# Scan of the latents: ScalarE writes x times D into the place of y head by head, and VectorE adds both directions to it

## The chip, the cores and the metric

The kernel runs on one core of a Trainium2 chip. The core has TensorE for matrix products (PE in the profile), VectorE (DVE), ScalarE (ACT), GpSimd (POOL) and SyncE (SP, here only an issuer of DMAs). Each engine works through its own list of instructions in order, and they wait for each other on semaphores. The metric is the device time of one execution in microseconds. Three runs of the kernel before took 1609.01 to 1610.98 us, with a median of 1609.97 us.

## The reference, cut to what matters

The model is one layer of a hybrid backbone: attention and a bidirectional state-space scan (Mamba-2) on one projection, then a gated merge and an MLP. 128 context tokens and 512 latent tokens go through it. The change concerns the scan of the latents. For each head the scan gives, per direction, a part within a chunk of 128 tokens and a part that comes from the state carried into the chunk; both directions and a skip term are then summed:

```python
y_diag = einsum('bcgij,bcgrij,bcjgr,bcjgrp->bcigrp', cb, decay, dt, x)
y_off  = einsum('bcign,bcigr,bcgrpn->bcigrp', Cm, exp(acs), h_prev)
y = y_f + flip(y_b) + d_skip[:, None] * xs      # 32 heads of 64 channels
y = rms_norm(y * silu(z), ssd_norm)
```

`d_skip` has one number for each head; `xs` is the convolved x.

## The kernel before, in words

Tokens lie on the 128 partitions in five tiles: chunk 0 is the context, chunks 1 to 4 are the latents. A chunk has 32 heads of 64 channels, so y is 128 x 2048; it is worked on in four quarters q of 8 heads (128 x 512), and each quarter has two groups g of four heads, g = 0 to 7.

The backward states of the latents are made first, and then the loops of the latents run, one on each engine, with c from 1 to 4. TensorE's loop multiplies the scan's small products between pieces of the big input projection (`fill`, with 24 matrix products for a piece), which need no result of the scan. The lists `F_LAT` and `F_LAT_G` (lines 370 and 371) say by hand how many pieces stand where: two ahead of the groups, and `[1, 0, 1, 0, 1, 1, 1, 1]` ahead of groups 0 to 7. For every group, TensorE runs `scan_group(g)` (line 1127): at an even g first `states` (what the carried states give, forward into PSUM bank tp 2 and backward into tp 3, and the new state), which waits until VectorE has read the last quarter's banks (`carried_ok`); then the four heads' product within the chunk, which waits for the group's weights (`m_ok`).

ScalarE makes for each group the decays (`exps`, line 1680): eight Relu instructions of 128x128, one for each head and direction, then the issue of a DMA that fetches the decay sums of the group after the next, and one Exp over 128x1024. `exps(n)` waits for its DMA and for TensorE to be done with group n-2, whose buffer it takes. In turn g it runs `weights(F_LAT_G[g])`, then `exps` of group g+2. `weights` (line 1652) takes a finished piece out of PSUM and, when the piece is the last of a weight block, splits the next block's weights (`split_hi`, line 1465: one Copy of 128x2048, that rounds to a high part). VectorE follows with `split_lo` (line 1958), which makes the low part from that high part.

VectorE's turn g is: `weighted(g)` (two instructions, lines 2236 and 2237: decays times C·B, then the sum of both directions, which gives `m_ok`); `weights`, whose first act is a `split_lo` that is owed; and at odd g `scaled` (x times dt for the next quarter), `carried` (line 2241) and `combined` (line 2266: adds the part within the chunk). `carried` multiplies the two directions' banks by their decays, updates the forward state `hF`, and adds x times D, for which `skipped` (line 2263) first multiplies x by `dsk` in the scratch tile `tq`. The helper `do` (line 1953) issues an instruction and waits for its end before the next one starts. `gated` multiplies a quarter of y by the gate, and ScalarE's `squares` sums its squares.

The names of most tiles appear in the trace as `arena`, since they are parts of one big tile.

Of the kernel before, what the change touches and what calls it, by code (L numbers as in the profile page):

```python
# [8 lines left out]
ACT = mybir.ActivationFunctionType  # L9
ALU = mybir.AluOpType  # L10
# [7 lines left out]
NT = (CTX + LAT) // P  # L18
HQ, HKV, HD = 8, 2, 128
DI = 2 * D  # L20
NH, SP_ = 32, 64
# [36 lines left out]
def count(sem, step=1, start=0):  # L58

    return {"sem": sem, "step": step, "base": start, "k": 0, "round": None, "per": 0}  # L60


def value(c, back=0):

    v = c["step"] * (c["base"] + c["k"] - back)
    assert v > 0, "a wait stands where there is something to wait for"
    return v if c["round"] is None else c["round"] * (c["per"] * c["step"]) + v


def step(c, n=1):  # L70

    c["k"] += n
    return c["step"]


def due(c, back=0):

    step(c)
    return value(c, back)
# [27 lines left out]
def build(nc, a, outs):  # L107
# [16 lines left out]
    with ExitStack() as ctx:  # L124
        def sb(n, shape, dt=F32):
            return ctx.enter_context(nc.sbuf_tensor(n, shape, dt))
# [17 lines left out]
        dec = sb("dec", [P, NT, 3, 2 * NH])  # L144
# [6 lines left out]
        dsk = sb("dsk", [P, NH])  # L151
# [10 lines left out]
        class Carve:  # L162
# [66 lines left out]
        hF = c5(NH, SP_)  # L229
        hB = c5(NH, SP_)  # L230
        yy = c5(NH, SP_)
# [9 lines left out]
        tq = c5(8, SP_)  # L241
# [7 lines left out]
        xs, bnx, ctx_t = (xs0, xs1), (bn0, bn1), (ct0, ct1)  # L249
# [3 lines left out]
        yz = zc.rearrange("p (h q) -> p h q", q=SP_)  # L253
# [59 lines left out]
        tp = ctx.enter_context(nc.psum_tensor("tp", [P, 4, 512], F32))  # L313
# [17 lines left out]
            pv_ready att_hi att_ok att_in av_in  # L331
            gat_in0 gat_in1 gat_ok ast_out0 ast_out1 xs_in0 xs_in1 bn_in0 bn_in1 bt_in ct_in0 ct_in1 abc_in0 abc_in1 sq_in sq_ok
            hb_in0 hb_in1 dsk_in h0_in h0_turned h0_ok zt_ok zq_in0 zq_in1 yc_in
            cb_ready cb_ok fall_ok e_ok m_ok xd_ok group_ready states_ready carried_ok quad_ok
            hb_out1 hb_out2 st_copied st_out kout_ok qk_turned qk_copied p_turned p_copied back_ready
            back_ok xwb_ok mod_copied pad_ok var_ok dev_ok y_out0 y_out1 yr_out0 yt_in0 yt_in1 yt_ok y_turned y_hi y_ok
            gm_in0 gm_in1 gb_ok merge_sum
# [2 lines left out]
        s = {n: ctx.enter_context(nc.semaphore(n)) for n in names}  # L340
# [53 lines left out]
        def block_done(p):  # L394

            if p < N_ZP:
                return p // NT if p % NT == NT - 1 else None
            return DI // BW + (p - N_ZP) // 4 if (p - N_ZP) % 4 == 3 else None
# [1060 lines left out]
        def _(act):  # L1459
# [5 lines left out]
            def split_hi(slot):  # L1465

                act.wait_ge(raws[slot]["sem"], due(raws[slot]))
                act.activation(whi[:, slot], raw[:, slot], ACT.Copy).then_inc(hi["sem"], step(hi))  # L1468
# [8 lines left out]
            def out_of_acc(dst, src, func):  # L1477

                act.wait_ge(ready["sem"], due(ready))
                act.activation(dst, src, func).then_inc(free["sem"], step(free))  # L1480
# [171 lines left out]
            def weights(n):  # L1652

                for p in range(pieces["k"], pieces["k"] + n):
                    b = block_done(p)
                    if p < N_ZP:
                        z = zo[p % NT // 3]
                        if p % NT in (0, 3):
                            step(z)
                            act.wait_ge(z["sem"], value(z, 1))  # L1660
                        act.wait_ge(ready["sem"], due(ready))
                        act.activation(zst[:, p % NT], acc[:, p % 2, 0:BW], ACT.Tanh, scale=0.5).then_inc(s["zt_ok"], 1)
                    else:
                        u, half = (p - N_ZP) // 2, p % 2
                        if half == 0:
                            if u == 0:
                                for z in zo:
                                    act.wait_ge(z["sem"], value(z))
                            step(go[u % 2])
                            act.wait_ge(go[u % 2]["sem"], value(go[u % 2], 1))  # L1670
                        out_of_acc(gst[:, u % 2, half * HALF:(half + 1) * HALF], acc[:, half, 0:HALF], ACT.Copy)
                    if b is not None:
                        split_hi(b % 2)
                step(pieces, n)

            falls, e_ok, quad, stc = (count(s[n]) for n in ("fall_ok", "e_ok", "states_ready", "st_copied"))
            sqi, sqo = count(s["sq_in"]), count(s["sq_ok"])
            flat = lambda t: t.rearrange("p h q -> p (h q)")

            def exps(n):  # L1680


                b, c, g = n % 2, n // NG, n % NG
                act.wait_ge(s[f"abc_in{b}"], 16 * (n // 2 + 1))
                if n >= 2:
                    act.wait_ge(s["group_ready"], n - 1)
                for d in range(2):
                    for r in range(R):
                        h = d * NH + R * g + r
                        last = act.activation(ee[:, b, d, r], abc[:, b, d, r], ACT.Relu, bias=dta[:, c, h:h + 1], scale=-1.0)  # L1690
                last.then_inc(falls["sem"], step(falls))
                act.wait_ge(falls["sem"], value(falls))
                if n + 2 < NT * NG:
                    decays_in(n + 2)
                act.activation(ee[:, b], ee[:, b], ACT.Exp, bias=kmx[:, c:c + 1], scale=-1.0).then_inc(e_ok["sem"], step(e_ok))  # L1695
# [6 lines left out]
            def squares(c, q, junk):  # L1702
# [3 lines left out]
                act.activation(junk, flat(y)[:, q * 512:(q + 1) * 512], ACT.Square,  # L1706
                               accum_out=ysq[:, c, q:q + 1]).then_inc(sqo["sem"], step(sqo))

            weights(2)
            heads_out(4)  # L1710
            act.wait_ge(s["rot_ok"], 5)
# [30 lines left out]
            for c in range(1, NT):  # L1742
                exps(NG * c)
                weights(1)
                if c > 1:
                    squares(c - 1, 2, zq[:, 0])
                exps(NG * c + 1)
                weights(1)
                if c > 1:
                    squares(c - 1, 3, zq[:, 1])  # L1750
                weights(F_LAT[c - 1] - 2)
                for g in range(NG):
                    weights(F_LAT_G[g])
                    if g + 2 < NG:
                        exps(NG * c + g + 2)
                    if g in (4, 6):
                        squares(c, g // 2 - 2, zq[:, g // 2 % 2])
            for q in (2, 3):
# [47 lines left out]
            for n in range(N_SCORE + HKV):  # L1806
# [7 lines left out]
                if n - 1 in GATED:  # L1814
                    q = GATED[n - 1]
# [132 lines left out]
        def _(dve):  # L1948
# [4 lines left out]
            def do(ins):  # L1953

                ins.then_inc(dv["sem"], step(dv))
                dve.wait_ge(dv["sem"], value(dv))
# [10 lines left out]
            for buf in (hf[:, :, CTX:CTX + 2], hf[:, :, NCONV:TP]):  # L1967
                last = dve.memset(buf, 0.0)
# [235 lines left out]

            xin_, (cbr, cbo, e_ok, m_ok) = pair("xs_in"), (count(s[n]) for n in ("cb_ready", "cb_ok", "e_ok", "m_ok"))
            xd, grp_q, quad, qok = (count(s[n]) for n in ("xd_ok", "group_ready", "states_ready", "quad_ok"))
            car, sqi = count(s["carried_ok"]), count(s["sq_in"])
            zqin = [count(s[f"zq_in{b}"], 16) for b in range(2)]
            flat = lambda t: t.rearrange("p h q -> p (h q)")
            v = lambda bank: bank.rearrange("p (h q) -> p h q", q=SP_)  # L2210
            f4 = lambda t, q: over(t[:, 8 * q:8 * q + 8], 8, SP_)
            banks = lambda q: (acc[:, 2], acc[:, 3]) if q % 2 == 0 else (tp[:, 0], tp[:, 1])
# [28 lines left out]
            def carried(c, b, q):  # L2241
                h = slice(8 * q, 8 * q + 8)
                dve.wait_ge(quad["sem"], due(quad))
                if q == 0:

                    for name, n in ((("h0_ok", 8),), (("hb_out2", 16),), (("y_out1", 16), ("sq_ok", 4)),
                                    (("y_out0", 16), ("sq_ok", 8)))[c - 1]:
                        dve.wait_ge(s[name], n)
                y = y_of(c)
                dve.tensor_tensor(y[:, h], v(tp[:, 2]), f4(dec[:, c, 0], q), ALU.mult)  # L2250
                if c < NT - 1:
                    do(dve.tensor_tensor(tq, v(tp[:, 3]), f4(dec[:, c, 0, NH:], q), ALU.mult))
                    dve.tensor_tensor(hF[:, h], hF[:, h], f4(dec[:, c, 2], q), ALU.mult)
                    do(dve.tensor_tensor(y[:, h], y[:, h], tq, ALU.add))
                    dve.tensor_tensor(hF[:, h], hF[:, h], v(banks(q)[1]), ALU.add).then_inc(car["sem"], step(car))
                else:
                    dve.tensor_tensor(tq, v(tp[:, 3]), f4(dec[:, c, 0, NH:], q), ALU.mult).then_inc(car["sem"], step(car))
                    dve.wait_ge(car["sem"], value(car))
                    do(dve.tensor_tensor(y[:, h], y[:, h], tq, ALU.add))
                skipped(b, q)  # L2260
                do(dve.tensor_tensor(y[:, h], y[:, h], tq, ALU.add))

            def skipped(b, q):
                do(dve.tensor_tensor(tq, xs[b][:, 8 * q:8 * q + 8], f4(dsk[:], q), ALU.mult))
# [42 lines left out]
            for j, c in ((1, 4), (2, 3), (3, 2)):  # L2307
# [13 lines left out]
                for q in range(4):  # L2321
                    if q < 3:
                        back_scaled(q + 1)
                    h = slice(8 * q, 8 * q + 8)
# [7 lines left out]
            for c in range(1, NT):  # L2332
                b, y = (c + 1) % 2, y_of(c)
# [4 lines left out]
                for g in range(NG):  # L2338
# [4 lines left out]
                    if g % 2 == 1:  # L2343
                        q = g // 2
# [332 lines left out]
```

## Time and profile before

| | |
|---|---|
| runs, median | 1609.97 us |
| the profiled execution | 1611.04 us |
| its span | 1609.3 us |
| PE busy | 1547.8 us (96%) |
| VectorE busy | 970.8 us (60%) |
| ScalarE busy | 616.4 us (38%) |

The span is from the first to the last instruction of the profiled execution; 1.7 us of its time lie around it. A busy share is an average over stages with different limits. The latents' loops, with the change in them, run from about 555 to 764 us, or 13% of the span.

### The profile page before, as it was taken

How to read it: one execution, taken by the hardware profiler on the slowest of the kernel's cores; microseconds unless marked ns; L12 is line 12 of the kernel's file. 1: busy time of each engine (PE TensorE's matmuls, PEld its weight loads, DVE VectorE, ACT ScalarE, POOL GpSimd, SP SyncE). 2: the span in 40 equal slices, each digit the busy share in tenths (PEclk: the TensorE clock that was granted, in tenths of full speed). 3: DMA queues.
4: the chain of work that ended last, by engine and by line, in shares of the span. 5: the costliest groups of instructions: out<-in, count | busy, mean ns of one | idle time of the engine just before them, and what ended most of it. 6: DMA issues, size and time to landing. Idle time of an engine off the chain costs nothing.

```text
span 1609.3 us, 27077 instructions
## 1 busy us (share of the span) xinstructions
PE 1547.8 (96%) x11130; PEld 1471.6 (91%) x11130; DVE 970.8 (60%) x1359; ACT 616.4 (38%) x1112; POOL 98.8 (6%) x155
## 2 busy tenths in 40 slices
PE   4999999999999999999999999999999999999997
PEld 2999999999999988988656899999999999999997
DVE  4666566668665698898465453447863343442478
ACT  2443333343563366767465342333421121221120
POOL 1011122100101100000000000000000000000000
PEclk9999999999999999999999999999999999999999
DMA  9555555542868678775700345324122222123221
GB/s 318 165 175 196 169 179 169 178 161 92 283 181 293 227 224 285 229 215 177 275 27 23 130 147 196 125 79 177 53 80 79 79 79 79 54 79 105 79 80 66
DMA packets 159910, 241.62 MB, mean 150 GB/s; under 512 B 8080, under 2 KB 126592, under 8 KB 156736
## 3 DMA queue, kind: packets, MB, share of 16 engines
q1 hardware_dynamic: 136624, 171.45, 32.2%
q0 software_dynamic: 12304, 47.72, 8.2%
q10 hardware_dynamic: 10880, 20.97, 5.0%
q8 instruction: 78, 1.28, 0.3%
q14 instruction: 24, 0.20, 0.0%
HBM read 195.06 MB, written 45.06 MB: 149 GB/s over the span
## 4 chain that ended last, share of the span: by engine, by line
PE 86%; DVE 6%; ACT 4%; SPq 1%; issue 1%; DMA 1%; ACTq 0%; DVEq 0%
PE acc L845 69%; PE tp L845 13%; PE tp L1251 1%; ACT arena L1690 1%; SPq L431 1%; DVE wlo L1961 1%; PE tp L941 1%; DMA arena<-in_w_mod 1%; ACT whi L1468 1%; ACT whi L1827 1%; DVE wlo L2418 1%; PE tp L1298 1%; DVE arena L2236 0%; PE tp L1016 0%; ACT arena L1695 0%
## 5 line engine op out<-in xcount | busy, mean ns | idle before, releaser
L845 PE MATMUL acc<-hh,whi 128*128 128x322 f32 x1152 | 297.9, 319 | 6.2 <-issue 4.2
L845 PE MATMUL acc<-hl,whi 128*128 128x322 f32 x1152 | 291.9, 314 | 0.0
L845 PE MATMUL acc<-hh,wlo 128*128 128x322 f32 x1152 | 290.9, 313 | 0.0
L845 PEld LDWEIGHTS acc<-hh,whi 128*128 128x128 f32 x1152 | 202.3, 192 | 10.6 <-issue 8.2
L1961 DVE TENSOR_TENSOR wlo<-raw,whi 128x2048 fp32r<-128x2048 f32 x74 | 169.4, 2289 | 62.7 <-ACT whi L1468 62.7
L1468 ACT ACTIVATE whi<-raw 128x2048 fp32r<-128x2048 f32 x74 | 141.1, 1907 | 163.7 <-PE acc L845 161.9
L845 PEld LDWEIGHTS acc<-hl,whi 128*128 128x128 f32 x1152 | 203.8, 192 | 0.0
L845 PEld LDWEIGHTS acc<-hh,wlo 128*128 128x128 f32 x1152 | 203.5, 192 | 0.0
L845 PE MATMUL acc<-whi,hh 128*128 128x256 f32 x640 | 183.1, 286 | 0.0
L845 PE MATMUL acc<-whi,hl 128*128 128x256 f32 x640 | 179.9, 281 | 0.0
L845 PE MATMUL acc<-wlo,hh 128*128 128x256 f32 x640 | 179.8, 281 | 0.0
L845 PE MATMUL acc<-whi,fl 128*128 128x256 f32 x560 | 157.2, 281 | 0.0
L845 PE MATMUL acc<-wlo,fh 128*128 128x256 f32 x560 | 157.2, 281 | 0.0
L845 PE MATMUL acc<-whi,fh 128*128 128x256 f32 x560 | 156.8, 280 | 0.0
L845 PE MATMUL tp<-arena 128*32 128x256 f32 (+4 forms) x774 | 135.1, 374 | 13.1 <-DVE arena L2237 11.2
L2067 DVE SCALAR_TENSOR_TENSOR arena<-arena,colp 128x642 f32<-128x642 f32 x128 | 113.6, 888 | 16.9 <-DVE arena L2065 1.2
L845 PEld LDWEIGHTS acc<-whi,hh 128*128 128x128 f32 x640 | 120.6, 188 | 0.6 <-issue 0.2
L845 PEld LDWEIGHTS tp<-arena 128*128 128x128 f32 (+1 forms) x774 | 88.1, 165 | 35.7 <-DVE arena L2237 12.9
L845 PEld LDWEIGHTS acc<-wlo,hh 128*128 128x128 f32 x640 | 120.5, 188 | 0.2
L845 PEld LDWEIGHTS acc<-whi,hl 128*128 128x128 f32 x640 | 120.5, 188 | 0.0
L845 PE MATMUL acc<-arena 128*128 128x64 f32 (+4 forms) x472 | 93.5, 414 | 20.4 <-DMA arena<-in_w_mod 11.6
L1690 ACT ACTIVATE arena<-arena,dta 128x128 f32<-128x128 f32 x320 | 97.8, 391 | 27.0 <-PE acc L845 16.4
(278 smaller groups left out, 2677.4 us busy)
## 6 DMA issues: line engine op xcount, KB each, us to landing
raw<-in_w_in SPq DMA_DIRECT2D x38, 1024.0 KB, 8.6
raw<-in_w_mlp SPq DMA_DIRECT2D x32, 1024.0 KB, 5.3
arena<-in_w_mod SPq DMA_DIRECT2D x24, 1024.0 KB, 8.2
arena<-decay_sums_t ACTq DMA_DIRECT2D x40, 512.0 KB, 6.2
arena<-xs_nat SPq DMA_DIRECT2D x8, 1024.0 KB, 10.9
raw<-in_w_ssd_o SPq DMA_DIRECT2D x8, 1024.0 KB, 6.1
y_nat<-arena POOLq DMA_DIRECT2D x6, 1024.0 KB, 6.0
arena<-y_nat SPq DMA_DIRECT2D x6, 1024.0 KB, 6.0
```

Of the source, the lines that this page charges most:

```text
L431: sp.dma_start(mod0[:, r], w_mod[:, :, r * BW:(r + 1) * BW]).then_inc(s[f"mod_in{r}"], 16)
L845: return pe.matmul(out, l, r, start=first, stop=last)
L941: last = pe.transpose(dst, cvs[:, n % 2, tok(t):tok(t) + P], ident)
L1251: last = pe.transpose(tp[:, j // 4, (j % 4) * P:(j % 4 + 1) * P], pr[:, u, j * P:(j + 1) * P], ident)
L1298: last = pe.transpose(tp[:, j, i * P:(i + 1) * P], yst[:, n % 2, c:c + P], ident)
L1468: act.activation(whi[:, slot], raw[:, slot], ACT.Copy).then_inc(hi["sem"], step(hi))
L1690: last = act.activation(ee[:, b, d, r], abc[:, b, d, r], ACT.Relu, bias=dta[:, c, h:h + 1], scale=-1.0)
L1827: last = act.activation(whi[:, slot, k], raw[:, slot, k], ACT.Copy, scale=colp[:, n:n + 1])
L1961: dve.tensor_tensor(wlo[:, slot], raw[:, slot], whi[:, slot].bitcast(F32), ALU.subtract).then_inc(lo["sem"], step(lo))
L2067: ins = dve.scalar_tensor_tensor(o, x[:, t:t + NCONV], w(t), o, ALU.mult, ALU.add)
L2418: last = dve.scalar_tensor_tensor(wlo[:, slot, k], raw[:, slot, k], colp[:, n:n + 1], whi[:, slot, k].bitcast(F32), ALU.mult, ALU.subtract)
```

## The change

ScalarE gets a function `begun(c, q)`: eight Copy activations of 128x64, each with the head's `dsk` column as its scale, write x times D straight into the quarter's place in y. It stands ahead of the groups for quarter 0 and, for quarters 1 to 3, at the end of turns 1, 3 and 5, behind the `exps` of groups 3, 5 and 7. The waits that guard y against its earlier use move with it from VectorE to ScalarE. VectorE's `carried` now puts both directions' products through `tq` and adds them to y, after a wait for `skip_ok`. The product `skipped` stays for the context alone.

```diff
+            def begun(c, q):
+                if q == 0:
+                    act.wait_ge(s[f"xs_in{(c + 1) % 2}"], 16 * ((c + 5) // 2))
+                    for name, n in ((("h0_ok", 8),), (("hb_out2", 16),), (("y_out1", 16), ("sq_ok", 4)),
+                                    (("y_out0", 16), ("sq_ok", 8)))[c - 1]:
+                        act.wait_ge(s[name], n)
+                y = yz if c % 2 else yy
+                for h in range(8 * q, 8 * q + 8):
+                    last = act.activation(y[:, h], xs[(c + 1) % 2][:, h], ACT.Copy, scale=dsk[:, h:h + 1])
+                last.then_inc(skips["sem"], step(skips))
...
                 weights(F_LAT[c - 1] - 2)
+                begun(c, 0)
                 for g in range(NG):
                     weights(F_LAT_G[g])
                     if g + 2 < NG:
                         exps(NG * c + g + 2)
+                    if g in (1, 3, 5):
+                        begun(c, (g + 1) // 2)
...
             def carried(c, b, q):
                 dve.wait_ge(quad["sem"], due(quad))
-                if q == 0:
...
-                dve.tensor_tensor(y[:, h], v(tp[:, 2]), f4(dec[:, c, 0], q), ALU.mult)
                 if c < NT - 1:
-                    do(dve.tensor_tensor(tq, v(tp[:, 3]), f4(dec[:, c, 0, NH:], q), ALU.mult))
-                    dve.tensor_tensor(hF[:, h], hF[:, h], f4(dec[:, c, 2], q), ALU.mult)
-                    do(dve.tensor_tensor(y[:, h], y[:, h], tq, ALU.add))
-                    dve.tensor_tensor(hF[:, h], hF[:, h], v(banks(q)[1]), ALU.add).then_inc(car["sem"], step(car))
-                else:
-                    dve.tensor_tensor(tq, v(tp[:, 3]), f4(dec[:, c, 0, NH:], q), ALU.mult).then_inc(car["sem"], step(car))
-                    dve.wait_ge(car["sem"], value(car))
-                    do(dve.tensor_tensor(y[:, h], y[:, h], tq, ALU.add))
-                skipped(b, q)
+                    do(dve.tensor_tensor(hF[:, h], hF[:, h], f4(dec[:, c, 2], q), ALU.mult))
+                do(dve.tensor_tensor(tq, v(tp[:, 2]), f4(dec[:, c, 0], q), ALU.mult))
+                dve.wait_ge(skips["sem"], due(skips))
+                do(dve.tensor_tensor(y[:, h], y[:, h], tq, ALU.add))
+                tb = dve.tensor_tensor(tq, v(tp[:, 3]), f4(dec[:, c, 0, NH:], q), ALU.mult)
+                if c < NT - 1:
+                    tb = dve.tensor_tensor(hF[:, h], hF[:, h], v(banks(q)[1]), ALU.add)
+                tb.then_inc(car["sem"], step(car))
+                dve.wait_ge(car["sem"], value(car))
                 do(dve.tensor_tensor(y[:, h], y[:, h], tq, ALU.add))
```

## Rows read from the trace of the kernel before

**Rows 1.** Busy time by stage; the stages are latent chunks 1 to 4.
```profile
core 0: us, PE busy (x) PEld busy (x) DVE busy (x) ACT busy (x) POOL busy (x), PEclk, DMA share, GB/s
555.20:609.30 54.10, 50.85 (x338) 49.10 (x336) 47.83 (x66) 36.49 (x87) 3.16 (x5) 0.94 0.71 216
609.30:662.90 53.60, 50.19 (x324) 48.22 (x322) 47.63 (x60) 37.16 (x91) 2.72 (x5) 0.97 0.76 244
662.90:716.70 53.80, 48.59 (x322) 46.61 (x322) 46.93 (x59) 37.21 (x91) 2.70 (x5) 1.00 0.78 256
716.70:761.40 44.70, 41.42 (x268) 39.75 (x266) 38.45 (x45) 32.13 (x82) 1.62 (x3) 0.96 0.64 191
```

**Rows 2.** Who waited for whom, PE, 560 to 770 us: total, times, longest.
```profile
PE tp L845 <- DVE arena L2237: 10.6, 5, 3.0
PE acc L845 <- DVE arena L2237: 2.8, 3, 1.1
PE tp L845 <- DVE arena L2255: 1.8, 2, 1.7
```

**Rows 3.** Timeline of PE in chunk 3: start, duration, then idle before and its releaser.
```profile
684.08 1.10 PE L845 MATMUL tp<-arena 128*128 128x64 f32 x8 [2.42 <-DVE arena L2237]
...
690.49 1.10 PE L845 MATMUL tp<-arena 128*128 128x256 f32 x4 [1.68 <-DVE arena L2255]
...
694.43 1.10 PE L845 MATMUL acc<-arena 128*128 128x64 f32 x8 [1.11 <-DVE arena L2237]
```

**Rows 4.** Timeline of ACT in chunk 3.
```profile
678.02 2.43 ACT L1690 ACTIVATE arena<-arena,dta 128x128 f32<-128x128 f32 x8
...
680.90 1.15 ACT L1695 ACTIVATE arena<-arena,ysc 128x1024 f32<-128x1024 f32 x1 [0.44 <-ACT arena L1690]
...
682.27 1.90 ACT L1468 ACTIVATE whi<-raw 128x2048 fp32r<-128x2048 f32 x1
```

**Rows 5.** Timeline of DVE in chunk 3, from the split to group 4.
```profile
684.20 2.29 DVE L1961 TENSOR_TENSOR wlo<-raw,whi 128x2048 fp32r<-128x2048 f32 x1 [0.18 <-ACT whi L1468]
...
687.01 0.68 DVE L2250 TENSOR_TENSOR arena<-tp,dec 128x512 f32<-128x512 f32 x1
...
689.66 0.69 DVE L2255 TENSOR_TENSOR arena<-arena,tp 128x512 f32<-128x512 f32 x1
690.26 0.68 DVE L2264 TENSOR_TENSOR arena<-arena,dsk 128x512 f32<-128x512 f32 x1
690.98 0.69 DVE L2261 TENSOR_TENSOR arena<-arena 128x512 f32<-128x512 f32 x1
...
692.42 1.22 DVE L2236 TENSOR_TENSOR arena<-arena 128x1024 f32<-128x1024 f32 x1
```

**Rows 6.** Who waited for whom, DVE, 560 to 770 us.
```profile
DVE arena L2236 <- ACT arena L1695: 10.1, 8, 1.9
...
DVE wlo L1961 <- ACT whi L1468: 0.5, 3, 0.2
```

**Rows 7.** Timeline of DVE in chunk 1, ahead of group 3.
```profile
574.52 0.42 DVE L2198 SCALAR_TENSOR_TENSOR arena<-arena,acc 128x256 f32<-128x256 f32 x1 [1.84 <-ACT arena L1662]
```

**Rows 8.** Timeline of DVE in chunk 4, from the carried part to group 4.
```profile
739.12 0.68 DVE L2250 TENSOR_TENSOR arena<-tp,dec 128x512 f32<-128x512 f32 x1
...
743.34 1.22 DVE L2236 TENSOR_TENSOR arena<-arena 128x1024 f32<-128x1024 f32 x1
```

**Rows 9.** Who waited for whom, ACT, 560 to 770 us.
```profile
ACT arena L1690 <- PE acc L845: 14.1, 5, 3.0
...
ACT arena L1690 <- DMA arena<-decay_sums_t: 10.1, 5, 3.0
```

**Rows 10.** Groups of ACT by line and shape: busy, mean ns, idle before.
```profile
L1690 ACT ACTIVATE arena<-arena,dta 128x128 f32<-128x128 f32 x320 | 97.8, 391 | 27.0 <-PE acc L845 16.4 <-DMA arena<-decay_sums_t 10.1 <-PE tp L845 0.5
...
L1827 ACT ACTIVATE whi<-raw,colp 128x256 fp32r<-128x256 f32 x64 | 26.5, 496 | 52.4 <-PE acc L845 39.7 <-DMA raw<-in_w_ssd_o 12.8
...
L1603 ACT ACTIVATE arena<-tp 128x128 f32<-128x128 f32 x10 | 2.8, 282 | 0.2 <-PE tp L1016 0.2
```

**Rows 11.** Busy time and granted clock behind the longest wait, in chunk 1.
```profile
580.00:583.00 3.00, 3.00 (x13) 3.00 (x13) 2.93 (x6) 2.56 (x9) 0.00 (x0) 0.50 0.69 185
```

More of the change, by code:

```diff
@@ L333, in build @@
             hb_in0 hb_in1 dsk_in h0_in h0_turned h0_ok zt_ok zq_in0 zq_in1 yc_in
-            cb_ready cb_ok fall_ok e_ok m_ok xd_ok group_ready states_ready carried_ok quad_ok
+            cb_ready cb_ok fall_ok e_ok m_ok xd_ok group_ready states_ready carried_ok quad_ok skip_ok
             hb_out1 hb_out2 st_copied st_out kout_ok qk_turned qk_copied p_turned p_copied back_ready
@@ L1707, in squares @@
                                accum_out=ysq[:, c, q:q + 1]).then_inc(sqo["sem"], step(sqo))
+            skips = count(s["skip_ok"])
+            def begun(c, q):
[8 more added lines that the diff above has]
+                last.then_inc(skips["sem"], step(skips))
             weights(2)
@@ L2206, in _ @@
             xd, grp_q, quad, qok = (count(s[n]) for n in ("xd_ok", "group_ready", "states_ready", "quad_ok"))
-            car, sqi = count(s["carried_ok"]), count(s["sq_in"])
+            car, sqi, skips = count(s["carried_ok"]), count(s["sq_in"]), count(s["skip_ok"])
             zqin = [count(s[f"zq_in{b}"], 16) for b in range(2)]
@@ L2243, in carried @@
                 dve.wait_ge(quad["sem"], due(quad))
-                if q == 0:
-                    for name, n in ((("h0_ok", 8),), (("hb_out2", 16),), (("y_out1", 16), ("sq_ok", 4)),
-                                    (("y_out0", 16), ("sq_ok", 8)))[c - 1]:
-                        dve.wait_ge(s[name], n)
                 y = y_of(c)
-                dve.tensor_tensor(y[:, h], v(tp[:, 2]), f4(dec[:, c, 0], q), ALU.mult)
                 if c < NT - 1:
-                    do(dve.tensor_tensor(tq, v(tp[:, 3]), f4(dec[:, c, 0, NH:], q), ALU.mult))
-                    dve.tensor_tensor(hF[:, h], hF[:, h], f4(dec[:, c, 2], q), ALU.mult)
-                    do(dve.tensor_tensor(y[:, h], y[:, h], tq, ALU.add))
-                    dve.tensor_tensor(hF[:, h], hF[:, h], v(banks(q)[1]), ALU.add).then_inc(car["sem"], step(car))
-                else:
-                    dve.tensor_tensor(tq, v(tp[:, 3]), f4(dec[:, c, 0, NH:], q), ALU.mult).then_inc(car["sem"], step(car))
-                    dve.wait_ge(car["sem"], value(car))
-                    do(dve.tensor_tensor(y[:, h], y[:, h], tq, ALU.add))
-                skipped(b, q)
+                    do(dve.tensor_tensor(hF[:, h], hF[:, h], f4(dec[:, c, 2], q), ALU.mult))
[7 more added lines that the diff above has]
+                dve.wait_ge(car["sem"], value(car))
                 do(dve.tensor_tensor(y[:, h], y[:, h], tq, ALU.add))
```

## The prediction

> **What bounds the kernel now.** I read the page's busy shares first: PE is busy for 96% of the span, so a change in the scan can move the end only where PE waits, or where its clock is low because it had waited. Next come the stages of the latents [rows 1]. In a chunk of 54 us PE is busy 49 to 51 us, VectorE 47 to 48 us and ScalarE 37 us: VectorE has little room, ScalarE more, and nearly all its waits are for PE or for a DMA. The list of who waited for whom then gives the whole of PE's waiting there: 10.6 + 2.8 + 1.8 = 15.2 us [rows 2], with VectorE as the releaser each time, and no others. The timeline of chunk 3 shows where they lie: 2.42 us ahead of group 3's product, 1.68 us ahead of quarter 2's states (for the banks that VectorE reads at L2255), and 1.11 us ahead of group 4's product [rows 3]. Chunks 1, 2 and 4 have the same first wait (up to 3.0 us), chunks 2 and 4 the last one as well.
>
> What stands behind each wait decides the case. Ahead of group 3 it is ScalarE's two `exps` in a row; VectorE waits up to 1.9 us for their Exp [rows 6], then gives PE the weights. Behind it VectorE's next act is the `split_lo` that it owes. This one starts at 684.20 after a wait of 0.18 us for ScalarE's `split_hi` [rows 5], which had started at 682.27, right behind the Exp that ended at 680.90 + 1.15 = 682.05 [rows 4]. So high split, low split, carried part and weights of group 4 are one chain without slack, through ScalarE and VectorE to PE's second and third waits. It occurs in three chunks: VectorE waits for that split 3 times, 0.5 us in all [rows 6]. These are chunks 2, 3 and 4. In chunk 1 the piece at that place is a z piece, and VectorE must multiply it before it weighs group 3: it waits 1.84 us for ScalarE's Tanh of that piece [rows 7], which stands behind the same Exp.
>
> **The change part by part.** *Added on ScalarE:* 4 chunks x 4 quarters x 8 = 128 activations of 128x64 with a pointer operand for the scale. The trace has none of this width. Two kinds with a pointer operand are near: 391 ns for 128 elements and 496 ns for 256 [rows 10], that is 0.82 ns an element. Eight of 128 elements stand in 2.43 us [rows 4], so one starts (2.43 - 0.39) / 7 = 0.291 us behind the other; 64 elements fewer take 0.052 us off, which leaves 0.239 us, and 8 x 0.239 = 1.9 us for a `begun`. The upper bound is the 128-wide pace itself, 8 x 0.291 = 2.3 us. The lower bound is the 282 ns copy without a pointer operand [rows 10], less the same overlap of 0.391 - 0.291 = 0.100 us and the same 0.052 us: 0.13 us, 1.0 us for a `begun`. I take 1.9 us, since the nearest rows share the operand. In all ScalarE gets 16 x 1.9 = 31 us of work.
>
> *Where these lie.* `begun(c, 0)` comes ahead of group 0, where ScalarE has waits soon after: it can push the next piece out by half a microsecond, and then ScalarE waits up to 3.0 us for PE before `exps` of group 2 [rows 9]. It costs nothing; without that cover it would be 1.9 us. `begun(c, 2)` and `begun(c, 3)` stand behind the `exps` of groups 5 and 7. Ahead of groups 4 and 6 ScalarE waits for its decay DMA, 10.1 us over five times [rows 9], which takes up a part, and behind them PE has a piece of its own ahead of each of the groups 4 to 7. I follow chunk 3: weights of groups 6 and 7 come some 1.2 us later, PE itself by then 1.4 us. Cost nothing; if that cover failed, 1.9 us each.
>
> `begun(c, 1)` is the one that counts. It goes in behind the `exps` of group 3 and ahead of turn 2's `weights`, just between the Exp that ends at 682.05 and the `split_hi` of 682.27. In chunks 2, 3 and 4 it shifts `split_hi`, and `split_lo` behind it, by 1.9 us. In chunk 1 it shifts the Tanh, the multiplication, group 3's weights and so PE's first wait by 1.9 us.
>
> *Removed on VectorE:* one 128x512 product a quarter, L2264, 690.26 to 690.98 = 0.72 us from start to start; one without a wait behind it takes 689.66 to 690.26 = 0.60 us [rows 5]. Now the carried part of a quarter is seven instructions in 687.01 to 691.70, as three at 0.60 or 0.61 and four at 0.71 to 0.73. The new order is six, five at 0.72 and one at 0.60: 4.2 us instead of 4.7, so 0.5 us less ahead of group 4 (692.42 now). In chunk 4, where L2250 to L2236 takes 743.34 - 739.12 = 4.2 us [rows 8], five instructions become four, all with a wait behind them, and with `combined` they take 5 x 0.72 = 3.6 us: 0.6 us less. The release of the banks (`carried_ok`) still stands behind five instructions, three of them waited for rather than two: 0.1 us later, in chunk 4 0.8 us later, but what PE meets last is group 4's weights.
>
> *Waits and queues.* The wait for `skip_ok` sits 1.4 us inside `carried`; `begun(c, 1)` has ended over 4 us before, since the low split (2.29 us) comes in between. The moved waits (stores of y two chunks back, the backward state) are for transfers long landed. Behind the late low split SP holds back the load of a weight block and one of z, both used over 10 us later; POOL's stores wait for pieces that ScalarE takes out up to 3 us later, and TensorE's pieces for the buffer of two pieces back, with room. The decay DMA of a later `exps` is issued up to 1.9 us later, which is in the shifts above.
>
> *The sum.* With b for a `begun`: chunk 1 costs b (PE's wait for group 3 grows; VectorE's 0.5 us is not met by a wait of PE), chunks 2 and 3 b - 0.5 each, chunk 4 b - 0.6. In all 4b - 1.6 = 6.0 us; by the bounds of b, 1.0 and 2.3 us, it is 2.4 and 7.6 us.
>
> *The clock.* Behind the longest wait PE runs at a granted clock of 0.50, the 1.2 GHz level, through 3 us of full work and more [rows 11]. By the mean clock of the stages [rows 1] the loss is (1 - 0.94) x 54.1 = 3.2 us in chunk 1, 1.6 in chunk 2, none in chunk 3 and 1.8 in chunk 4, behind first waits of 3.0, 2.15, 2.42 and 2.75 us. After the change chunk 1's wait is 4.9 us, and chunk 3 has 2.4 us, then 1.7 + 1.9 + 0.1 = 3.7 us and 0.6 us. I expect one further low stretch of the mean size, (3.2 + 1.6 + 1.8) / 3 = 2.2 us, and keep none and three as the ends (a low clock between groups 3 and 4 of chunks 2 to 4 costs nothing, as VectorE ends last there).
> The Trainium skill, TensorE: Matmul & The Clock Gate, section "What's actually happening", has throttling as the default state that activity releases. By that rule each of the four lengthened waits brings a low stretch of its own, and the sum would be 6.0 + 4 x 2.2 = 14.8 us; chunk 3, which keeps a clock of 1.00 through 2.42, 1.68 and 1.11 us of waiting, speaks for fewer.
> A second page speaks against the change: the Trainium skill, ScalarE: Activation LUTs, section "Rules for kernel authors", gives multiplications to VectorE. Here 0.72 us of VectorE turn into 1.9 us of ScalarE, so the trace agrees on the engines' time; the page does not say that ScalarE's place in the chain makes it a loss.
>
> Sum against the profiled execution: 1611.04 (span 1609.3) + 6.0 + 2.2 = 1619.2 us. That execution was 1.1 us above the median of the runs, so in their terms 1609.97 + 8.2 = 1618.2 us. PE has work in hand up to the end of the loops and little waiting behind them, so nothing takes a shift back.
>
> **The rivals.** *ScalarE becomes the bound.* With 4 x 1.9 = 7.6 us more a chunk it is busy 45 of 54 us [rows 1], and lateness from `begun(c, 2)` may reach the weights of groups 6 or 7. For it: in chunk 2 VectorE already waits for an Exp at group 7 (one of the 8 waits in [rows 6]). Against it: PE has pieces of 3.8 us ahead of each of these groups. Price: one more `begun` on the path in each chunk, 4 x 1.9 = 7.6 us on top, 1625.8 us.
> *VectorE's relief decides, not slower.* If a `begun` cost little enough to hide in front of the split, PE's third wait would shrink by what VectorE saves: 0.5 + 0.5 + 0.6 = 1.6 us, 1608.4 us; with VectorE the bound in every quarter, 12 x 0.5 + 4 x 0.6 = 8.4 us, 1601.6 us. For it: VectorE ends each of PE's waits [rows 2]. Against it: ScalarE has no slack ahead of the split (0.18 us). It decides from b below 0.5 us, under half of my lower bound.
> *Hidden anyway.* Where PE's clock is low, the piece ahead of quarter 2's states is longer and takes up the wait, and other waits shrink as PE shifts: 1610 to 1612 us. Against it: group 4's weights come behind the states and depend on VectorE alone.
>
> **How the numbers follow.** Forecast 0.72; ScalarE as the bound 0.13; hidden 0.08; relief 0.07, half of it a gain that counts. The measurement can tell 0.2%, 3.2 us. The forecast's own range is 2.4 us without the clock to 7.6 + 3 x 2.2 = 14.2 us, 1612.4 to 1624.2 us, a twelfth of it under 3.2 us. For 8 in 10 I take 1613 to 1625 us: it leaves out the two small cases and the upper half of the first rival. Faster 0.04, same 0.13, slower 0.83.
>
> **What would show it.** In the profile after: 128 activations with mean near 340 ns, eight in about 2.0 us; VectorE's wait for `split_hi` at L1961 up from 0.5 us over three times to about 6; in chunk 1 a wait for the Tanh of some 3.7 us; PE's waiting in the loops up from 15.2 to about 21 us; VectorE less busy by 16 x 0.68 = 11 us; mean clock of chunks 1 to 4 lower in one of them. The prediction is wrong if PE's waits ahead of groups 3 and 4 do not grow, if ScalarE's `exps` come late in groups 5 to 7 with PE waiting, or if an activation of 64 elements starts every 0.13 us.

## The result, and the profile after

The changed kernel takes 1616.29 us (median of 8 runs, 1613.31 to 1619.0) against 1609.83 us (8 runs, 1607.94 to 1610.98): ratio 1.004, 95% interval 1.0031 to 1.0048. It is 6.5 us slower; 1618.2 us had been predicted. The profiled execution took 1613.31 us with a span of 1611.6 us, so it is one of the shortest of the eight. The runs are spread over 5.7 us, where they were spread over 3.0 us before. The longer time gets its cause below; the wider spread did not come back when the kernel was run again, as the first experiment shows.

First, what ScalarE added. This is the group of the new instructions (line engine op, out<-in, shapes, count | busy, mean ns | idle before):

```profile
L1721 ACT ACTIVATE arena<-arena,dsk 128x64 f32<-128x64 f32 x128 | 32.1, 333 | 0.0
```

And this is ScalarE's timeline in chunk 3, the place of [rows 4]:

```profile
681.61 1.15 ACT L1695 ACTIVATE arena<-arena,ysc 128x1024 f32<-128x1024 f32 x1 [0.44 <-ACT arena L1690]
682.67 2.00 ACT L1721 ACTIVATE arena<-arena,dsk 128x64 f32<-128x64 f32 x8
684.58 0.41 ACT L1480 ACTIVATE arena<-acc 128x322 f32<-128x322 f32 x1
684.90 1.89 ACT L1468 ACTIVATE whi<-raw 128x2048 fp32r<-128x2048 f32 x1
```

The eight activations sit between the Exp and the high split, and take 684.58 - 682.67 = 1.91 us of the queue. VectorE's timeline at the same place shows who waits for that:

```profile
686.83 2.29 DVE L1979 TENSOR_TENSOR wlo<-raw,whi 128x2048 fp32r<-128x2048 f32 x1 [2.08 <-ACT whi L1468]
...
689.63 0.68 DVE L2264 TENSOR_TENSOR arena<-arena,dec 128x512 f32<-128x512 f32 x1
690.35 0.69 DVE L2265 TENSOR_TENSOR arena<-tp,dec 128x512 f32<-128x512 f32 x1
...
694.57 1.22 DVE L2254 TENSOR_TENSOR arena<-arena 128x1024 f32<-128x1024 f32 x1
```

The wait ahead of the low split went from 0.18 to 2.08 us [rows 5]. The carried part and `combined` now take 694.57 - 689.63 = 4.94 us; before they took 5.41 us (687.01 to 692.42), so VectorE's relief is 0.47 us. VectorE's and PE's lists of who waited for whom, 560 to 770 us:

```profile
DVE arena L2254 <- ACT arena L1695: 11.7, 8, 2.2
DVE arena L2247 <- PE tp L845: 8.8, 3, 3.4
DVE wlo L1979 <- ACT whi L1468: 6.2, 3, 2.1
DVE arena L2216 <- ACT arena L1662: 5.5, 2, 4.1
```

```profile
PE tp L845 <- DVE arena L2255: 12.3, 4, 5.3
PE tp L845 <- DVE arena L2270: 1.4, 2, 0.7
PE acc L845 <- DVE arena L2255: 1.3, 3, 0.5
```

In VectorE's list the wait for the high split is up from 0.5 to 6.2 us over the same three times [rows 6], and the wait for the Tanh of chunk 1, at most 1.84 us before [rows 7], is 4.1 us. PE's list is the surprise: 15.0 us in all, where it was 15.2 us [rows 2], though the loops got longer. The stages tell why. The first four rows are the changed kernel's latent chunks, each from the start of its first pair of pieces to that of the next; the last two lie within chunk 3, behind the first wait, and the columns are those of [rows 1]:

```profile
555.01:608.85 53.84, 48.58 (x323) 46.66 (x322) 44.20 (x59) 42.27 (x116) 3.16 (x5) 0.94 0.73 220
608.85:663.85 55.00, 51.73 (x323) 49.76 (x322) 45.58 (x56) 44.75 (x123) 2.70 (x5) 0.94 0.77 244
663.85:718.85 55.00, 51.59 (x323) 49.62 (x322) 44.90 (x55) 44.54 (x123) 2.71 (x5) 0.94 0.72 244
718.85:764.84 45.99, 42.93 (x267) 41.26 (x266) 36.05 (x41) 39.59 (x114) 1.62 (x3) 0.93 0.58 178
...
687.00:690.00 3.00, 3.00 (x13) 3.00 (x13) 3.00 (x3) 2.48 (x9) 0.00 (x0) 0.50 0.57 213
690.00:692.50 2.50, 2.49 (x13) 2.23 (x11) 2.40 (x5) 2.50 (x8) 0.00 (x0) 0.74 0.70 123
```

Cut at the same places, the four chunks took 52.48, 53.57, 53.84 and 44.69 us before; now it is 53.84, 55.00, 55.00 and 45.99 us, 5.25 us more. The span grew by only 2.3 us, since this execution reached chunk 1 earlier (at 555.01 against 556.81 us) and took 846.8 us behind the loops, where it was 847.9 us. Over all the kept traces chunk 1 starts between 554.96 and 557.03 us, with the same code ahead of it in all the changed ones, so these two parts vary from execution to execution.

In chunk 3 PE runs its piece at a granted clock of 0.50, the 1.2 GHz level, while VectorE is still busy with the late split. PE is then not idle but slow, and group 4's weights come no later for it: the wait has turned into busy time. The mean clock of chunk 3 fell from 1.00 [rows 1] to 0.94, so one further chunk than before has a low stretch; here it cost nothing. PE's row for the wait ahead of group 4 shows that a wait became busy time too. Here are its three waits of chunk 3, as in [rows 3]:

```profile
684.80 1.97 PE L845 MATMUL tp<-arena 128*128 128x64 f32 x8 [2.15 <-DVE arena L2255]
...
693.24 1.10 PE L845 MATMUL tp<-arena 128*128 128x256 f32 x4 [0.74 <-DVE arena L2270]
...
696.58 1.10 PE L845 MATMUL acc<-arena 128*128 128x64 f32 x8 [0.51 <-DVE arena L2255]
```

The second and third wait are shorter than before (1.68 and 1.11 us), and yet from the first of these rows to the last it is 11.78 us, where it was 694.43 - 684.08 = 10.35 us. What must be read is the distance between two fixed events, not the sum of the waits.

### The profile page after: what moved, and what is told of

The parts are those of the page before. It is cut to its first block, busy times and chain, and to the rows that moved or that the text cites. A ratio compares the mean times of both kernels' runs of the same rounds, so it can differ in the third digit from the quotient of the medians.

```text
span 1611.6 us, 27205 instructions
## 1 busy us (share of the span) xinstructions
PE 1548.4 (96%) x11130; PEld 1472.3 (91%) x11130; DVE 962.2 (60%) x1343; ACT 645.7 (40%) x1240; POOL 98.7 (6%) x155
## 4 chain that ended last, share of the span: by engine, by line
PE 86%; DVE 5%; ACT 5%; issue 1%; SPq 1%; DMA 1%; ACTq 0%; DVEq 0%
PE acc L845 69%; PE tp L845 13%; PE tp L1251 1%; ACT arena L1690 1%; SPq L431 1%; PE tp L941 1%; DMA arena<-in_w_mod 1%; ACT whi L1468 1%; DVE wlo L1979 1%; ACT whi L1845 1%; DVE wlo L2430 1%; PE tp L1298 1%; ACT arena L1721 0%; DVE arena L2254 0%; PE tp L1016 0%
## 5 line engine op out<-in xcount | busy, mean ns | idle before, releaser
L845 PEld LDWEIGHTS acc<-whi,fh 128*128 128x128 f32 x560 | 105.5, 188 | 0.0
```

Of the source, the lines that this page charges most:

```text
L845: return pe.matmul(out, l, r, start=first, stop=last)
```

## The experiments

All times are medians, each beside runs of the kernel before on the same chip; the difference given is the one of the two medians. "The loops" are PE's four chunks, cut as above (204.6 us before).

**The changed kernel again.** No edit.

> The changed kernel once more, beside the others of this call. Theory (the eight activations ahead of the high split of turn 2 lie on the path): 5 to 7 us above before, the loops of the latents 5.2 us longer as in its first profile. No rival differs here; the run sets the scale for the others.

1615.38 us against 1609.93 us, ratio 1.0028 (1.0019 to 1.0038): 5.4 us slower, within what was expected. But its loops in the profile are 213.1 us, 8.5 us longer and not 5.2. The same program gave both, so they can be laid side by side. Here are PE's products of chunk 2 for quarter 2's states and group 4 in this execution, behind the piece; then the stages of the clock in chunk 2, behind the wait of 2.15 us for group 3, first this execution, then the changed kernel's first profile:

```profile
638.20 1.10 PE L845 MATMUL tp<-arena 128*128 128x256 f32 x4 [3.72 <-DVE arena L2270]
639.14 0.79 PE L845 MATMUL acc<-arena 128*128 128x256 f32 x2
639.72 1.92 PE L845 MATMUL tp<-arena 128*128 128x256 f32 x4
```

```profile
632.00:635.00 3.00, 2.48 (x17) 2.21 (x15) 3.00 (x3) 2.46 (x8) 0.00 (x0) 1.00 0.69 273
635.00:638.00 3.00, 0.00 (x0) 0.00 (x0) 2.90 (x5) 2.98 (x8) 0.00 (x0) 1.00 0.93 280
638.00:641.00 3.00, 2.80 (x10) 2.35 (x11) 2.86 (x5) 2.56 (x8) 0.00 (x0) 0.73 1.02 307
641.00:644.00 3.00, 3.00 (x16) 2.73 (x15) 2.97 (x5) 1.69 (x8) 0.00 (x0) 0.70 0.97 334
```

```profile
632.00:635.00 3.00, 3.00 (x13) 3.00 (x12) 3.00 (x3) 2.45 (x8) 0.00 (x0) 0.50 0.72 286
635.00:638.00 3.00, 2.63 (x13) 2.36 (x11) 2.90 (x5) 2.79 (x7) 0.00 (x0) 0.72 0.92 261
638.00:641.00 3.00, 2.76 (x12) 2.20 (x12) 2.86 (x5) 2.56 (x7) 0.00 (x0) 1.00 1.10 368
```

Here PE did its piece at full clock, was done at 634.5 us, stood idle for 3.72 us and then got the low clock for the states and group 4, which VectorE waits for and PE needs next: chunk 2 took 55.90 us. In the first profile the low clock fell on the piece, ahead of a wait that was due anyhow: 55.00 us. In chunk 4 the low clock fell on the piece behind group 4 (5.34 us instead of 3.81), which nothing hides either. That is 0.9 us in chunk 2, 0.9 in chunk 3 and 1.5 in chunk 4, 3.3 us together, and the two spans differ by 3.5 us. VectorE's waits for the high split and the Tanh are the same in both (6.2 us, and 4.1 us in chunk 1). The wide spread of the first eight runs is not explained by that alone: these nine runs of the changed kernel lie within 2.8 us, the 27 beside them of the kernel before within 6.2 us.

**The activations of quarter 1 moved to where ScalarE waits.**

```diff
                 for g in range(NG):
                     weights(F_LAT_G[g])
+                    if g == 0:
+                        begun(c, 1)
                     if g + 2 < NG:
                         exps(NG * c + g + 2)
-                    if g in (1, 3, 5):
+                    if g in (3, 5):
                         begun(c, (g + 1) // 2)
```

> The eight activations for quarter 1 are moved from behind the exps of group 3 to turn 0, ahead of the exps of group 2, where ScalarE waits 2.1 to 3.0 us for PE; everything else as changed. Theory: the whole loss goes and VectorE's relief of 0.5, 0.5 and 0.6 us in chunks 2, 3 and 4 is left: 1.6 us below before (about 1608.2). Rival 'ScalarE as the bound' (its 31 us of added work cost wherever they stand): the loss stays, 5 us or more above before.

1607.36 us against 1609.93 us, ratio 0.998 (0.997 to 0.9991): 2.6 us faster than before, 8 us faster than the changed kernel, with the same instructions. The loops are 203.5 us. ScalarE's and VectorE's timelines of chunk 3 in this run:

```profile
670.08 2.01 ACT L1721 ACTIVATE arena<-arena,dsk 128x64 f32<-128x64 f32 x8
673.12 2.45 ACT L1690 ACTIVATE arena<-arena,dta 128x128 f32<-128x128 f32 x8 [1.03 <-PE acc L845]
```

```profile
683.25 2.29 DVE L1981 TENSOR_TENSOR wlo<-raw,whi 128x2048 fp32r<-128x2048 f32 x1 [0.17 <-ACT whi L1468]
```

The activations end with 1.03 us to spare before PE lets the `exps` of group 2 go, and the low split waits 0.17 us again. The rival "ScalarE as the bound" is out: some 30 us of added work on ScalarE (616.4 to 646.1 us busy), and no loss. Of the 2.6 us the loops show 1.05 (203.53 against 204.58 us).

**VectorE's part alone.** `begun` is not called; `carried` keeps its new order, without its wait for `skip_ok`, and takes back the waits that guard y.

```diff
-                begun(c, 0)
...
-                    if g in (1, 3, 5):
-                        begun(c, (g + 1) // 2)
...
-                dve.wait_ge(skips["sem"], due(skips))
```

> VectorE's part alone: carried in its new order, without the wait for the skip term, and ScalarE without the 128 activations. Leaves out the term x times D of the latents (y keeps what lay in its place). Theory: VectorE's relief reaches PE only ahead of group 4 of chunks 2, 3 and 4: 1.6 us below before. Rival 'VectorE is the bound in every quarter': 8 us below before. The order alone with a later release of the banks could cost 0.1 us a chunk, which shows at PE's wait for L2255's successor in chunk 3.

1608.38 us against 1609.93 us, ratio 0.9983 (0.9974 to 0.9992): 1.6 us faster, and far from the 8 us of the rival in which VectorE is the bound in every quarter. That this is also what the sum gave (0.5 + 0.5 + 0.6) is partly luck, since in the profile the loops are only 0.4 us shorter (204.16 us). In chunk 2 the relief is there: from group 3's product to group 4's it is 9.88 us, where it was 10.34. But PE then meets a new wait at the chunk's end, for VectorE's last sum, and VectorE had waited for the Exp of group 7:

```profile
652.52 1.23 DVE L2251 TENSOR_TENSOR arena<-arena 128x1024 f32<-128x1024 f32 x1 [2.24 <-ACT arena L1695]
660.17 1.02 PE L845 MATMUL tp<-arena 128*128 128x128 f32 x7 [0.44 <-DVE arena L2282]
```

ScalarE, ahead of the `exps` of group 6, had waited 3.24 us for its decay DMA. Before, VectorE's wait at that Exp was 1.23 us and PE had none there. In chunks 3 and 4 this execution has a low clock on the piece behind group 3, which hides the relief. So 16 instructions fewer on VectorE, in the new order, are a small gain, and a part of it meets the next wait.

**ScalarE's part alone.** The activations as changed, and VectorE's `carried` of before behind a wait for `skip_ok`.

```diff
             def carried(c, b, q):
                 dve.wait_ge(quad["sem"], due(quad))
+                dve.wait_ge(skips["sem"], due(skips))
                 y = y_of(c)
                 dve.tensor_tensor(y[:, h], v(tp[:, 2]), f4(dec[:, c, 0], q), ALU.mult)
...
                 skipped(b, q)
```

> ScalarE's part alone: the 128 activations as changed, VectorE's carried as before (it waits for skip_ok first and then overwrites y, with its own product by D). Theory: four times 1.9 us without VectorE's relief, so 0.5 to 0.6 us in each of chunks 2 to 4 more than the changed kernel: 1.6 us above it, 7 to 8 us above before. Rival 'VectorE's new order is what costs' (three waited operations ahead of the bank release): equal to before.

1617.92 us against 1609.93 us, ratio 1.0044 (1.003 to 1.0058): 8.0 us slower, where four times 1.91 us make 7.6. It is 2.5 us above the changed kernel beside it, where 1.6 were expected; the 0.9 us between them is less than the 3.3 us by which two executions of one kernel differed above, but no run shows that the clock made it.

**Twice as much ahead of the split.** Quarter 2's activations come up to those of quarter 1.

```diff
-                    if g in (1, 3, 5):
+                    if g in (1, 5):
                         begun(c, (g + 1) // 2)
+                    if g == 1:
+                        begun(c, 2)
```

> The activations of quarter 2 are moved up from behind the exps of group 5 to right behind those of quarter 1, so 16 stand ahead of the high split of turn 2; the sum of the work is the same. Theory (4b - 1.6 us, with b the time ahead of the split, now 3.8 us): 7.6 us above the changed kernel, 13 us above before, give or take 3 us of clock. Rival 'ScalarE's added work costs wherever it stands': equal to the changed kernel.

1625.83 us against 1609.98 us, ratio 1.0084 (1.0067 to 1.01): 15.9 us slower, at the upper edge of the 13 us "give or take 3". The wait for the high split is 12.0 us over three times, twice 6.2. PE's list, 560 to 770 us:

```profile
PE tp L845 <- DVE arena L2257: 14.2, 4, 7.2
PE tp L845 <- DVE arena L2272: 8.2, 2, 4.1
PE tp L845 <- DVE arena L2270: 2.2, 1, 2.2
```

The waits are now long, up to 7.2 us, and low stretches come on top of them: chunks 1 and 3 run at a mean clock of 0.91. In chunk 2, behind 4.08 us of waiting, four of the states' products took 1.91 us; at the full clock they take 1.03. By the medians the first 1.9 us ahead of the split cost 5.4 us, with the relief of 1.6 us already in it, and the next 1.9 us cost 10.5 us more, where time alone gives 4 x 1.9 = 7.6 us. How much of the excess is the clock depends on the execution that it is held against: the loops of 220.5 us are 10.7 us longer than in the changed kernel's first profile, but 7.4 us longer than in its second.

**One copy instead of eight for quarter 1.**

```diff
-                for h in range(8 * q, 8 * q + 8):
-                    last = act.activation(y[:, h], xs[(c + 1) % 2][:, h], ACT.Copy, scale=dsk[:, h:h + 1])
+                if q == 1:
+                    last = act.activation(y[:, 8:16], xs[(c + 1) % 2][:, 8:16], ACT.Copy)
+                else:
+                    for h in range(8 * q, 8 * q + 8):
+                        last = act.activation(y[:, h], xs[(c + 1) % 2][:, h], ACT.Copy, scale=dsk[:, h:h + 1])
```

> Quarter 1 alone is written by one Copy of 128x512 in place of eight of 128x64 with a scale; it leaves out the factor D in quarter 1. b falls from 1.9 to about 0.5 us. Theory: 4 x 0.5 - 1.6 = 0.4 us above before, 5 us below the changed kernel. Rival 'ScalarE's total': 0.2 of the loss goes, about 4 us above before.

1609.81 us against 1609.98 us, ratio 0.9994 (0.9985 to 1.0003): no difference that can be told, where 0.4 us were expected. ScalarE goes on 0.52 us behind the start of this one Copy:

```profile
681.25 0.61 ACT L1721 ACTIVATE arena<-arena 128x512 f32<-128x512 f32 x1
681.77 0.42 ACT L1480 ACTIVATE arena<-acc 128x322 f32<-128x322 f32 x1
```

So the 512 elements are at most 0.52 us of the 1.91, and the rest comes from having eight instructions, each with a pointer operand; the run does not part the eight starts from the eight pointers.

**Only quarter 1.** The other quarters' activations are cut to one head each.

```diff
-                for h in range(8 * q, 8 * q + 8):
+                for h in range(8 * q, 8 * q + (8 if q == 1 else 1)):
```

> The activations of quarters 0, 2 and 3 are cut from eight to one each (21 us of ScalarE's added work go; the skip term is left out for seven heads of eight there), those of quarter 1 stay. Theory: as the changed kernel, 5 to 6 us above before. Rival 'ScalarE as the bound': three quarters of the loss goes, 1 to 2 us above before.

1615.06 us against 1609.98 us, ratio 1.0027 (1.0018 to 1.0036): 5.1 us slower, like the changed kernel's 5.4 us, though ScalarE's busy time fell by 20 us (645.9 to 626.3 us). Seven eighths of the other 12 `begun` cost nothing that these runs can tell, which is to about 2 us.

**Behind the split.** `begun(c, 1)` stands in turn 2, after the piece and the high split.

```diff
                 for g in range(NG):
                     weights(F_LAT_G[g])
+                    if g == 2:
+                        begun(c, 1)
                     if g + 2 < NG:
                         exps(NG * c + g + 2)
-                    if g in (1, 3, 5):
+                    if g in (3, 5):
```

> The activations of quarter 1 stand in turn 2, behind the piece and the high split and ahead of the exps of group 4. Theory: the loss goes in chunks 2 to 4 as in the run with them in turn 0; in chunk 1 too, since the Tanh comes ahead. The exps of group 4 come up to 1.9 us later, and VectorE meets them only behind its split and carried part: 1.6 to 2.6 us below before. Rival: those exps are now what group 4 waits for, 2 us or more above the run with them in turn 0.

1607.78 us against 1609.98 us, ratio 0.9983 (0.9973 to 0.9993): 2.2 us faster, not to be told from the 2.6 us of the place in turn 0. One step down the queue is enough. The rival, that the `exps` of group 4 come too late, is out.

**Against the wait that is left.** In the kernel with quarter 1's activations in turn 0 PE still waits 10.4 us ahead of group 3. This one starts from that kernel and gives group 3 a piece, taken from group 7.

```diff
-        F_LAT_G = [1, 0, 1, 0, 1, 1, 1, 1]
+        F_LAT_G = [1, 0, 1, 1, 1, 1, 1, 0]
```

> As the run with the activations of quarter 1 in turn 0, and the piece that stood ahead of group 7 is moved ahead of group 3 (F_LAT_G from [1,0,1,0,1,1,1,1] to [1,0,1,1,1,1,1,0]), where PE waits 10.4 us over the four chunks. Theory (PE's wait ahead of group 3 is the chain of two exps, which a piece of 3.8 us covers, and the low clock comes from that wait): 8 to 12 us below the other run of this call, if PE has no new wait at group 7. Rival: group 7's weights end last, PE waits there as long as it did at group 3, and the time is the same within 2 us.

1622.12 us against 1610.38 us, ratio 1.0077 (1.0063 to 1.0092): 11.7 us slower. Both the theory and the rival missed. PE's list in this run:

```profile
PE tp L845 <- DVE arena L2284: 15.1, 3, 5.0
PE tp L845 <- DVE arena L2272: 2.8, 3, 1.5
PE acc L845 <- DVE arena L2257: 2.4, 4, 0.9
PE tp L845 <- DVE arena L2257: 0.9, 1, 0.9
```

The wait ahead of group 3 is gone, but PE now waits 5.0 us at the end of each of the first three chunks for L2284, VectorE's `combined`, which reads the banks that the next chunk's first products fill. The piece ahead of group 7 had covered VectorE's last carried part and both sums. The move did a second thing, which its trace shows at the end of chunk 1, ScalarE first:

```profile
594.66 2.00 ACT L1721 ACTIVATE arena<-arena,dsk 128x64 f32<-128x64 f32 x8
596.57 0.42 ACT L1480 ACTIVATE arena<-acc 128x322 f32<-128x322 f32 x1
596.89 1.90 ACT L1468 ACTIVATE whi<-raw 128x2048 fp32r<-128x2048 f32 x1
```

```profile
598.82 2.29 DVE L1981 TENSOR_TENSOR wlo<-raw,whi 128x2048 fp32r<-128x2048 f32 x1 [1.90 <-ACT whi L1468]
601.03 0.68 DVE L2266 TENSOR_TENSOR arena<-arena,dec 128x512 f32<-128x512 f32 x1
```

Every later piece has moved up by one, so the chunk's second pair of splits now comes one turn earlier, and VectorE makes its low split ahead of the last carried part. Without the move the low split came only in the next chunk (at 613.39 us in the first run of quarter 1 in turn 0). And `begun(c, 3)` now stands right ahead of a high split, as `begun(c, 1)` did in the changed kernel, and VectorE waits for it by the same 1.90 us. Of the 5.03 us ahead of chunk 2, 1.90 + 2.2 = 4.1 us are this wait and this split; that PE's wait would be near 0.9 us without them is an estimate. Whether another order of the pieces wins was not tried.

**Quarter 1 in turn 0 again**, beside that run.

> The kernel with the activations of quarter 1 in turn 0 once more, on the same chip as the run with the moved piece: 1.6 to 2.6 us below before.

1608.15 us against 1610.38 us, ratio 0.998 (0.9971 to 0.999): 2.2 us faster, with the same ratio as the first time. This version beats both kernels, and so does the one behind the split. Here the mean clock is 1.00 in chunk 3 and 0.96 in chunk 4, as it was before [rows 1], and the relief can be read off: from group 3's product to group 4's it is 9.87 us in chunks 2 and 3 and 7.95 us in chunk 4, which is 0.47, 0.48 and 0.60 us less than before. The loops as a whole are 0.8 us shorter (203.75 us), since chunk 2 gives its part back at its end:

```profile
661.32 0.91 PE L845 MATMUL tp<-arena 128*128 128x128 f32 x6 [0.91 <-DVE arena L2284]
```

## Why the prediction was right, step by step

The mechanism held: eight activations ahead of the high split delay the split, the carried part and the weights of group 4 in chunks 2 to 4, and in chunk 1 the Tanh and the weights of group 3. The time came out as close as it did partly because the clock's share happened to be small.

- **Price of a `begun`.** 1.9 us was taken from the slope of two wider groups [rows 10]; 1.91 us was measured, at 333 ns an instruction. The bounds of 1.0 and 2.3 us had not been needed. The Trainium skill, ScalarE: Activation LUTs, section "What ACT_TABLE_LOAD costs", gives 280 ns + 0.833 ns an element with one pointer operand and an overlap of 93 ns: by estimate from these, 333 ns, and 240 ns from start to start. This trace agrees to the nanosecond (333) and nearly so in the distance (0.239).
- **Place.** That `begun(c, 1)` alone counts holds within what the runs can tell: the run with only quarter 1 and the one with quarter 1 moved show the two halves of it. It holds for this order of the pieces; in the run with the moved piece `begun(c, 3)` is on the path.
- **Waits of VectorE.** The wait for the high split was to go to about 6 us and went to 6.2; the one for the Tanh to 3.7 us and went to 4.1.
- **Relief.** 0.5, 0.5 and 0.6 us in chunks 2 to 4: from group 3's product to group 4's it is now 1.44, 1.43 and 1.30 us longer, which is 1.91 less 0.47, 0.48 and 0.61. In chunk 1, 1.91 us more up to group 3's product (20.05 to 21.96 us from the chunk's start). These four make 6.1 us; the sum had 6.0. The second run of quarter 1 in turn 0 shows the relief by itself, 0.47, 0.48 and 0.60 us. What the sum left out is that in chunk 2 a shorter way to group 4 meets a wait at the chunk's end, so once the activations are out of the way PE keeps less than 1.6 us of it.
- **The clock, the term that was mis-sized.** "One further low stretch of the mean size", 2.2 us, was added as a constant. In the first profile the clock gave back: chunk 1's piece behind the long wait took 5.34 us, where it had taken 6.21, so chunk 1 cost 1.36 us and not 1.91; and the low stretches of chunks 2 to 4 hid. The loops: 6.1 - 0.6 - 0.3 = 5.2 us, the last 0.3 being in chunk 3, where a wait of 2.42 us ahead of group 3 was 2.15 us this time. In the second profile the clock cost 0.9 + 0.9 + 1.5 us more than that, 8.5 us in all. Against the sum's 6.0 us without the clock the medians gave 6.5 and 5.4 us, so on average the term is worth about nothing, and single executions lay 0.8 us below and 2.5 us above. One further low stretch did come, in chunk 3; what was mis-sized is its price. The prediction priced it at the mean of 2.2 us, while the same prediction had said that a low clock between groups 3 and 4 costs nothing. Hence 1618.2 instead of 1616. "None" as an end of the range held. The sum of 14.8 us, with a low stretch to pay behind each of the four lengthened waits, is out: even the loops of the second profile are only 8.5 us longer.
- **A sign that was wrong.** PE's waiting was to rise to 21 us. It did in the second profile (12.3 + 5.9 + 1.6 + 0.3 = 20.1 us), and fell to 15.0 in the first. The prediction had said that a low clock between groups 3 and 4 is hidden, but had not drawn from it that the waits would then not grow. One of its signs of being wrong, "if PE's waits ahead of groups 3 and 4 do not grow", is therefore half met in the first profile (group 3 of chunk 1 grew from 3.0 to 5.3 us, group 4 of chunk 3 fell from 1.11 to 0.51 us), although the cause was the one predicted. The sign was badly chosen: the distance from group 3's product to group 4's grew in every one of chunks 2 to 4.
- **VectorE's busy time** fell by 8.6 us (970.8 to 962.2), not 11, since with more waits fewer neighbours overlap in the busy count: the relief is 0.5 us a quarter, as the sum had it, and not the 0.68 us of one instruction.
- **The chances.** By the prediction's own parts "slower" was 0.72 x 11/12 + 0.13 = 0.79, and not the 0.83 that it gives.

## What to carry to other kernels

Before work is moved to an engine with room, find the place in that engine's queue, and ask what stands directly behind it: 23 us of new work cost nothing that could be told in twelve of sixteen places, and 1.9 us in each of the other four, 7.6 us, was set against a relief of 1.6 us. Shifting one call by one step in the queue turned 5 us lost into 2 us gained, with the same instructions. The place has to be looked up again when anything else in the queue moves: one moved piece put another call ahead of a split. Where the granted clock can fall, compare distances between fixed events in the two traces, since a wait can turn into slow busy time; and where it can, take a second profile of the same kernel before a microsecond is explained.

## What was not expected of the hardware

- The same wait has two prices. Behind a wait of 2.15 us in chunk 2, PE's clock was 0.50 from the first product on in one execution, and 1.00 for the whole next piece in another, where it fell only behind a second wait of 3.72 us. The Trainium skill, TensorE: Matmul & The Clock Gate, section "What's actually happening", has activity release the throttle; here the low stretches shown above did end under steady work, but the length of a wait did not say whether one would come: 2.42 us brought none in chunk 3 of the kernel before [rows 1], and 2.15 us did in chunk 3 after.
- More waiting can go with less clock loss: in chunk 1 the longest wait grew from 3.0 to 5.3 us, and the piece behind group 3 got faster, 6.21 to 5.34 us.
- Why an execution gets the one or the other was not settled. No run here sets the clock's timing, so it stays open.
